# Who asks for the expert matrices: ScalarE for gate and up, the synchronising engine for down

## The reference

```python
gp = softmax(ht @ w_group + b_group)              # 4 groups, the best one is taken
top_l, e_idx = top_k(logits of its 8 experts, 2)  # 2 experts a token, of 32
for wg, wu, wd, ge in experts:                    # 1024x256, 1024x256, 256x1024
    z = silu(ht @ wg) * (ht @ wu)
    acc = acc + ge[:, None] * (z @ wd)
```

## Time and profile before

| | |
|---|---|
| Time, median of 3 runs | 1284.18 us (1281.82 to 1286.32) |
| The profiled execution: its time, its span | 1284.24 us, 1282.5 us |
| TensorE busy | 1146.2 us, 89% of the span |
| VectorE, ScalarE, GpSimd busy | 520.0, 408.5, 224.8 us |
| q1 (SP's transfers) | 240.67 MB, 46.7% of 16 engines' span |
| q10 (ScalarE's), q0 (GpSimd's) | 8.39 MB, 21.00 MB |
| Chain that ended last | PE 60%, DMA 21%, DVE 8%, POOL 4% |

### The profile page before, as it was taken

The page is one execution under the profiler, slowest core; times in us unless marked ns, Lnnn a source line. Parts: engine busy times, 40 slices in busy tenths (PEclk is TensorE's granted clock), DMA queues, the critical chain, the costliest instruction groups (busy, mean ns, idle before and its releaser), DMA issues.

```text
span 1282.5 us, 29436 instructions
## 1 busy us (share of the span) xinstructions
PE 1146.2 (89%) x12656; PEld 616.6 (48%) x12656; DVE 520.0 (41%) x927; ACT 408.5 (32%) x787; POOL 224.8 (18%) x235
## 2 busy tenths in 40 slices
PE   5999999999999989899987867999999899997880
PEld 3355555555555644455544433444445455544440
DVE  6854554554555412511111104699942511111115
ACT  3335444444354312311111113466543311111112
POOL 2000000000000002122211110688801122211110
PEclk8999999999999999999999998999999999999995
DMA  5011011011012166699999976126201799999975
GB/s 169 3 52 60 9 50 39 21 55 40 19 56 90 50 223 256 240 418 426 424 423 427 426 317 262 66 98 274 103 1 25 274 406 426 423 425 425 425 333 221
DMA packets 50209, 271.95 MB, mean 212 GB/s; under 512 B 16386, under 2 KB 19586, under 8 KB 31648
## 3 DMA queue, kind: packets, MB, share of 16 engines
q1 hardware_dynamic: 38048, 240.67, 46.7%
q0 software_dynamic: 10880, 21.00, 4.4%
q10 hardware_dynamic: 1152, 8.39, 1.6%
HBM read 263.73 MB, written 23.07 MB: 224 GB/s over the span
## 4 chain that ended last, share of the span: by engine, by line
PE 60%; DMA 21%; DVE 8%; POOL 4%; ACT 3%; SPq 2%; issue 2%; POOLq 0%; DVEq 0%; ACTq 0%
PE psum L1269 14%; DMA big<-in_moe_w_gate_up_dram 12%; PE psum L841 9%; PE psum L1770 9%; PE psum L1431 6%; DMA conv_w<-in_moe_w_gate_up_dram 6%; PE psum L854 4%; POOL big L1993 4%; DVE psum L2147 2%; PE psum L2021 2%; SPq L355 2%; DVE h L944 2%; PE psum L1420 1%; PE psum L1548 1%; PE psum L1572 1%
## 5 line engine op out<-in xcount | busy, mean ns | idle before, releaser
L841 PE MATMUL psum<-big 128*64 128x256 f32 x1728 | 216.4, 394 | 42.6 <-DMA big<-in_moe_w_gate_up_dram 31.3
L1269 PE MATMUL psum<-big 128*128 128x512 f32 x384 | 192.6, 622 | 4.8 <-ACT big L1303 2.9
L841 PEld LDWEIGHTS psum<-big 128*64 128x64 f32 x1728 | 120.0, 140 | 124.7 <-DMA big<-in_moe_w_gate_up_dram 43.1
L915 DVE TENSOR_TENSOR big<-big,psum 128x128 f32<-128x128 f32 x64 | 18.4, 288 | 325.7 <-ACT big L882 325.7
L781 POOL DMA_INDIRECT chosen<-big x64 | 63.8, 996 | 347.8 <-ACT big L892 157.9
L854 PE MATMUL psum<-big 128*64 128x512 f32 x512 | 120.8, 592 | 1.2 <-ACT big L887 1.2
L1770 PE MATMUL psum<-big 128*128 128x512 f32 x256 | 114.4, 599 | 0.8 <-ACT big L2116 0.8
L2021 PE MATMUL psum<-big,conv_w 128*128 128x512 f32 x256 | 110.4, 593 | 2.2 <-ACT big L415 1.2
L1993 POOL TENSOR_TENSOR big<-big 128x512 f32<-128x512 f32 x81 | 103.1, 1273 | 42.0 <-ACT big L2095 31.5
L754 POOL TENSOR_SCALAR big<-big 128x1024 f32<-128x1024 f32 x4 | 11.4, 2856 | 547.4 <-PE psum L462 547.3
L1613 ACT COPY big<-psum 128x512 f32<-128x512 f32 (+1 forms) x112 | 68.6, 650 | 118.4 <-PE psum L1431 116.5
(11 more groups left out here) (256 smaller groups left out, 1305.1 us busy)
## 6 DMA issues: line engine op xcount, KB each, us to landing
big<-in_moe_w_gate_up_dram SPq DMA_DIRECT2D x54, 2048.0 KB
big<-in_moe_w_down_dram SPq DMA_DIRECT2D x64, 1024.0 KB, 32.7
conv_w<-in_moe_w_gate_up_dram SPq DMA_DIRECT2D x10, 2048.0 KB
big<-in_rwkv_w_rkv_dram SPq DMA_DIRECT2D x24, 512.0 KB, 4.1
conv_w<-in_conv_w_pw_dram SPq DMA_DIRECT2D x8, 1024.0 KB, 4.7
big<-chosen ACTq DMA_DIRECT2D x8, 1024.0 KB, 7.9
big<-in_rwkv_w_o_dram SPq DMA_DIRECT2D x4, 1024.0 KB, 8.8
rows<-big POOLq DMA_DIRECT2D x8, 512.0 KB, 6.3
```

Source lines behind the costliest of these rows:

```text
L841: last = nc.tensor.matmul(o[half * SLOTS:(half + 1) * SLOTS, 0:F_EXP].rearrange("p (u f) -> p u f", u=2), m.xT[e // 2 % 2][:, c, (e % 2) * ...
L1269: last = nc.tensor.matmul(bank[b], m.w[:, n, c, :], x[:, c, :], start=(c == 0), stop=(c == C - 1))
```

## The change

The body of `sp_load_up` becomes `load_up(m, eng, e)`, with the asking engine as an argument. In `sp_moe_weights` the first round's loop asks for down matrices alone. In `act_moe`, `silu(e)` asks for the gate and up matrices of expert e + 6, behind the wait for expert e's product that it has anyway, as long as e + 6 is an expert. In further rounds SP asks for the gate and up matrices of the first six experts (the refill over the end of a round) and for all down matrices, ScalarE for the other 26.

```diff
+        def load_up(m, eng, e):
+            n, j = m.layer * N_EXP + e, e % RING
+            eng.dma_start(m.up[j], a["moe_w_gate_up"][n]).then_inc(m.up_in[j], 16)
+
         def sp_load_up(m, sp, e):
-            n, j = m.layer * N_EXP + e, e % RING
-            sp.dma_start(m.up[j], a["moe_w_gate_up"][n]).then_inc(m.up_in[j], 16)
+            load_up(m, sp, e)
...
         def sp_moe_weights(m, sp):
-            for e in range(RING, N_EXP + 1):
-                if e < N_EXP:
-                    sp.wait_ge(m.gate_up_done, FREE2 + e - RING + 1)
-                    sp_load_up(m, sp, e)
-                if e > RING:
-                    sp.wait_ge(m.down_done, FREE2 + e - 1 - RING + 1)
-                    sp_load_down(m, sp, e - 1)
+            for e in range(RING, N_EXP):
+                sp.wait_ge(m.down_done, FREE2 + e - RING + 1)
+                sp_load_down(m, sp, e)
...
                     for e in range(N_EXP + 1):
-                        if e < N_EXP:
+                        if e < RING:
                             sp.wait_ge(m.gate_up_done, N_EXP * r + (FREE2 + user_before(e) + 1))
                             sp_load_up(m, sp, e)
...
                 def silu(e):
                     act.wait_ge(m.gate_up_done, N_EXP * r + (FREE2 + e + 1))
+                    if e + RING < N_EXP:
+                        load_up(m, act, e + RING)
                     act.wait_ge(m.z_ready, N_EXP * r + (e + 1))
                     nc.scalar.activation(m.silu[e % 2], bank[4 + e % 2][:, 0:P], ACT.Silu).then_inc(m.silu_ready, 1)
```

## The result

The changed kernel takes 1316.62 us, median of 4 runs (1314.18 to 1320.74), against 1285.08 us, the median of 4 runs of the kernel before; the ratio is 1.026, 95% interval 1.0233 to 1.0287. It is slower. The prediction said 1287.5 us, and 1279 to 1298 as its range. It was wrong by 29 us.

A forecast was written before the change was run, and what follows sets the result against it. The prediction took the expert stages to be bound by the DMA engines' backlog of weight loads, at 424 GB/s. Its only priced term, 2 x 1.8 = 3.6 us on 1284.2, gave 1287.8, stated as 1287.5 us; range 1279 to 1298.

The forecast's parts named there:

- Two queues: Expert stages: SP's and ScalarE's weight queues share engines packet by packet; only the last gate and up load suffers, 1.8 us a layer.
- rival B: Down loads run ahead if engines share by bytes or time; each stage ends some 7 us later; 1298 us, chance 0.12.
- The step's own term: End of each stage: down 30 served beside up 31, up to 2.5 us ahead of it; taken as 1.8 us a layer.
- Who asks: 26 gate and up loads a layer asked for by ScalarE before silu: cost nothing, hidden by `down` and the next product.
- a hanging request: ScalarE's queue: at most six loads outstanding, below the ten at which SP's queue hung; nothing hangs, nothing taken.
- C: ScalarE's requests hang if the room for ten loads is shared by both queues; 1301 us in all, chance 0.05.
- SP's order: SP waits only for `down_done`; down loads asked for at the same events or up to 8.6 us sooner.
- Rival A: No cost of order for the last loads of the expert stages: 1280.6 to 1284.9 us, chance 0.21.
- Rival D: More bandwidth: two queues keep the DMA engines fuller, 438 GB/s against 424; 1277 us, chance 0.12.
- The range: Whole kernel: 1279 to 1298 us, leaving out the cases of more bandwidth, hanging ScalarE requests and half of downs running ahead.
- The signs that the prediction named: SP's requests 0.33 us, ScalarE's 0.3 to 0.8, share 1.01 at 424 GB/s, down loads landing after some 20 us or more.

The follow-up runs named there:

- e3: Changed kernel with each weight load asked for in two halves (8 KB and 4 KB packets), same queues and askers: 1291.15 us, ratio 1.0059 to the kernel before.
- e5: Kernel before the change with each weight load asked for in two halves, all from SP: 1287.54 us, ratio 1.0042 to the kernel before.
- e7: Changed kernel with every second two of the sixteen gathers left out: 1275.70 us, ratio 0.9951 to the kernel before.
- e1: Changed kernel with all 52 loads of a stage asked for from ScalarE, none from SP: 1291.14 us, ratio 1.0047 to the kernel before.
- e8: Changed kernel with SP asking for gate and up loads in halves and ScalarE for whole down loads (8 KB packets both): 1302.31 us, ratio 1.0150 to the kernel before.
- e4: Changed kernel with GpSimd waiting for the landing of the scatter before the one it waited for: 1318.36 us, ratio 1.0268 to the kernel before.
- e2: Changed kernel with SP asking for both matrices of even experts and ScalarE of odd ones: 1318.21 us, ratio 1.0258 to the kernel before.
- e6: Changed kernel with only odd experts' gate and up loads from ScalarE, all other loads from SP: 1293.27 us, ratio 1.0081 to the kernel before.

## Why the prediction was wrong

*Step "Two queues" failed.* It read the earlier trace rows rightly, packet against packet whatever the size, but applied it to the two weight queues only. The row's own second partner, the gathers' queue, was not counted as a third taker of turns. The prediction counts that queue only as a share of the bandwidth (5.6 us instead of 4.9 in rival B), and names no need of packets, no wait of GpSimd and no `columns`; had it taken the 10880 packets of q0, less those of the stores, by pairs and engines, 19 against 18 would have stood there. The packets of q0 stood on the page of before; the 18 follow from a load's 128 partitions, eight to an engine, and its completion. The term was 0 in the sum and is 16 and 20 us in the two layers.

*The step's own term*, the companion of the last gate and up load, 1.8 us a layer: where starvation is taken away, it is part of what e3 has over its control e5, some 2 us in the kernel against 3.6 forecast; the intervals overlap, so neither this cost nor its absence is shown. In the changed kernel itself it does not arise, since weights are ahead.

*Who asks and a hanging request: right.* ScalarE's requests take 0.334 us and nothing hangs. In the changed kernel this proves little: loads land 21 to 23 us after they are asked for (medians), every 8.7 us on each queue, so about three stand on a queue and not six. In e7 six gate and up loads do, as TensorE waits there for a load with five more asked for behind it, and no request there takes longer than 0.40 us on ScalarE, 0.69 on SP. e1 shows that ScalarE's requests would hang with as many loads as SP had before. Its 7 us go with that, and with a flip that waits 14.2 us; no run takes the two apart. The prediction put 17 us on such hangs in C, which needed a room shared by the queues. The room is each queue's own: in e8 SP's requests hang, up to 5.5 us, while ScalarE's take at most 0.39. *SP's order* cost nothing that shows: TensorE waits for no weight.

*Rival A and the rule of the Trainium skill* ("DMA: Bandwidth & Descriptors", section "Issuing engines are not separate DMA queues") that several askers save only the time to ask: the changed kernel and e3 have the same askers and the same queues and differ by 25 us. The rule holds for bandwidth (421 to 426 GB/s from 600 to 640 us) and says nothing of a third queue's share.

*Rival B* is real where it is built (e8: 20 us, the halves' cost included, against 14), and not what happened. *Rival D* is out: 426 GB/s with three queues as with two.

*The range* was wrong for the same reason: no case in it had anything but the weights as what is late. The signs that the prediction named had the same gap. Requests of 0.33 us, a share of 1.01 at 423 GB/s until 613 us, down loads that land after 23.4 us and no wait for a down matrix all came, in a kernel 29 us slower than forecast; none of the signs looked at GpSimd's queue.

*A reading*: the slices at 9 tenths are 17 to 22, not 16 to 22, and slice 32 has 406 GB/s, outside "418 to 427". Nothing in the sum hangs on it.

## What to carry over

Before a stream is moved to a queue of its own, count for each queue that has work the packets per unit of work and DMA engine, small ones too, since a packet of under 512 B waited as long for its turn as one of 16 KB; the queue with the most packets set the pace here, and a new busy queue lengthened the turn of the others. In these runs one queue that keeps the order in which loads are used was worth more than a second asker, as long as the engine that asks may hang. Where two queues are needed, smaller weight packets give turns back: 25 us here, which is net of some 5 us that the halving costs.

## What the runs showed of the hardware

Three backlogged queues share the DMA engines by packets to within 1% (719, 720 and 722; 720 each in e4; 719 to 724 in e2), with packets of 16 KB, of 8 KB, and on the third queue more than half under 512 B. A queue of loads hangs its asker at about ten outstanding loads of nine packets an engine: SP in the kernel before, ScalarE in e1 (up to 7.95 us), and ScalarE with twelve half loads in e3 (7.8 us). Six whole loads on a queue did not (e7), nor did the nine at most that e6 has on SP's (its longest request took 0.63 us). Each queue has room of its own (e8: SP's requests hang up to 5.5 us, ScalarE's take at most 0.39). So the room does not go by bytes: twelve halves are no more bytes than six wholes, and only the halves hung (e3, and SP's in e5 and e8). Whether it goes by packets or by requests is open, as every load here, whole or half, has the same 144 packets.
